# Copies at a layer's feed-forward boundary moved to ScalarE's queue, a bias formed on GpSimd, and the first norm's sum one product later

## The reference

```python
def rmsnorm(x, g): return x * rsqrt(mean(x * x) + eps) * g
mkv_p = mem_kv_proj(mem_prompt, w_mem_kv[i])             # memory keys and values of the prompt
hp, hs = rmsnorm(xp, norm_mix_pre[i]), rmsnorm(xs, norm_mix_pre[i])
# compression of cached keys/values: blocks of 32 rows to one token, through a hidden layer of 128
bias = einsum('jce,jcef->cf', pe, w1) + b1               # 32 positions j, key/value c, 64 features e
hid  = proj[:, :-1, :, 0] + proj[:, 1:, :, 1] + bias
ckv  = einsum('bnhcf,cfe->bnhce', gelu(hid), w2)
xp = xp + rmsnorm(mp @ w_out[i], norm_mix_post[i])
xp = xp + rmsnorm(swiglu_ffn(rmsnorm(xp, norm_ffn_pre[i]), w_ffn_in[i], w_ffn_out[i]), norm_ffn_post[i])
```

## Time and profile before

| | |
|---|---|
| median of 3 runs | 1276.94 us (1275.72 to 1277.89) |
| profiled execution | 1279.42 us |
| its span, first to last instruction | 1277.6 us |
| mean granted TensorE clock | 0.952 of full |
| PE busy | 1170.9 us, 92% of the span |
| PEld, DVE, ACT, POOL busy | 837.0, 357.8, 230.7, 223.0 us |
| DMA | 185.65 MB, 145 GB/s on average |
| longest waits of PE | 12.2 us for a `fi` slab, 11.9 us in three for VectorE, 11.5 us in 17 for ScalarE |

### The profile page before, as it was taken

The page is one execution under the profiler, slowest core; times in us unless marked ns, Lnnn a source line. Parts: engine busy times, 40 slices in busy tenths (PEclk is TensorE's granted clock), DMA queues, the critical chain, the costliest instruction groups (busy, mean ns, idle before and its releaser), DMA issues. The chain is left out here.

```text
span 1277.6 us, 16640 instructions
## 1 busy us (share of the span) xinstructions
PE 1170.9 (92%) x6096; PEld 837.0 (66%) x6096; DVE 357.8 (28%) x780; ACT 230.7 (18%) x546; POOL 223.0 (17%) x297
## 2 busy tenths in 40 slices
PE   6999999999789999999999979987649899999996
PEld 5766666667667777777777753334537677777774
DVE  5428776410221111000331054326501321111002
ACT  2411000003210000000222045553301210001000
POOL 0008667510001000100000051302440010000000
PEclk9999999999989999999999869998778899999998
DMA  6835433412943434644422451445541143343342
GB/s 271 326 99 188 135 99 119 131 50 99 344 188 132 135 138 142 275 136 136 165 99 100 157 175 49 130 142 198 161 136 67 66 165 132 133 135 123 126 138 75
DMA packets 58532, 185.65 MB, mean 145 GB/s; under 512 B 8449, under 2 KB 39426, under 8 KB 47618
## 3 DMA queue, kind: packets, MB, share of 16 engines
q1 hardware_dynamic: 51890, 166.89, 38.0%
q0 software_dynamic: 6144, 12.59, 3.4%
q10 hardware_dynamic: 432, 5.24, 1.0%
HBM read 180.91 MB, written 10.02 MB: 149 GB/s over the span
## 5 line engine op out<-in xcount | busy, mean ns | idle before, releaser
L721 PE MATMUL banks<-normed,slabs 128*128 128x288 f32 x1408 | 347.6, 410 | 16.9 <-DMA slabs<-in_wfi 12.2
L721 PEld LDWEIGHTS banks<-normed,slabs 128*128 128x128 f32 x1408 | 270.4, 192 | 93.9 <-issue 17.7
L761 PE MATMUL banks<-hidden,slabs 128*128 128x288 f32 x704 | 171.2, 406 | 1.4 <-issue 1.4
L697 PE MATMUL banks<-arena,phase 128*128 128x384 f32 x512 | 171.0, 492 | 0.0
L761 PEld LDWEIGHTS banks<-hidden,slabs 128*128 128x128 f32 x704 | 133.6, 190 | 39.0 <-issue 2.3
L697 PEld LDWEIGHTS banks<-arena,phase 128*128 128x128 f32 x512 | 96.5, 191 | 65.1 <-issue 1.2
L1436 POOL TENSOR_TENSOR projected<-projected,rstd 128x288 f32<-128x288 f32 x44 | 34.9, 794 | 453.4 <-ACT projected L1208 453.4
L488 PE MATMUL banks<-normed,slabs 128*128 128x288 f32 (+1 forms) x416 | 106.7, 413 | 1.2 <-ACT normed L1141 1.2
L488 PEld LDWEIGHTS banks<-normed,slabs 128*128 128x128 f32 (+1 forms) x416 | 77.2, 189 | 25.6 <-issue 3.7
L1208 ACT ACTIVATE projected<-projected 128x288 f32<-128x288 f32 x44 | 19.5, 443 | 281.4 <-DVE projected L1555 281.4
L1508 DVE TENSOR_TENSOR normed<-normed 128x288 f32<-128x288 f32 x24 | 11.0, 458 | 199.1 <-ACT normed L1201 199.1
(11 more groups left out here) (306 smaller groups left out, 1118.7 us busy)
## 6 DMA issues: line engine op xcount, KB each, us to landing
slabs<-in_wfi SPq DMA_DIRECT2D x44, 1024.0 KB, 4.9
slabs<-in_w SPq DMA_DIRECT2D x25, 1024.0 KB, 4.7
arena<-in_cmp SPq DMA_DIRECT2D x128, 192.0 KB, 2.8
slabs<-in_wfo SPq DMA_DIRECT2D x32, 704.0 KB, 4.0
arena<-in_slck SPq DMA_DIRECT2D x64, 96.0 KB, 2.7
arena<-in_slck POOLq DMA_DIRECT2D x64, 96.0 KB, 2.6
out_win_old<-in_winold SPq DMA_DIRECT2D x1, 6096.0 KB, 22.4
arena<-in_slcv POOLq DMA_DIRECT2D x48, 96.0 KB, 2.6
```

The costliest lines, as they stand in the source:

```text
L697: ins = nc.tensor.matmul(out.rearrange("p h (g s) -> p h g s", s=8), W1S[:, c, a, j, :], PG[b % 2][:, :, c * 8 + j, :, :].rearrange("p g h ...
L721: return nc.tensor.matmul(BK[2 * (u % SLOTS) + c][:, 0:T], wt[:, k, c * P:c * P + P], Hn[:, k, :], start=(k == 0), stop=(k == KC - 1), ski ...
L761: ins = nc.tensor.matmul(BK[b][:, 0:T], wt[:, k, :], HD[:, 11 * kh + k, :], start=(kh + k == 0), stop=(kh * 11 + k == 21))
```

## The change

Three edits, and what they need:

1. `pre_sum(0)` is called after the third product of the memory projection, not after the second. ScalarE's root stands behind the first copy of slab 1.
2. GpSimd forms the position products: one product of 4096 elements, W1 times `pe` held constant over 128 elements, into `arena` 2048 to 6144, four additions that halve it, the last into `PER`. TensorE sums over partitions with two one-column products. ScalarE's copy of the row goes. SP waits for GpSimd before it loads the first pages, which land in the same part of `arena`.
3. The window copy and layer 1's memory keys and values are issued by ScalarE after the last copy of the S5 loop, in the order keys, values, values, window rows. In SP's list they are gone. SP's loop over the `fi` slabs is written out and issues the same loads.

```diff
+        PEP = AR[:, 2048:6144].rearrange("p (c q f) -> p c q f", c=2, q=16)
...
+        glu_in, pe_summed = sem("glu_in_ready"), sem("position_products_summed")
...                                              (mem_project, TensorE)
                         banks.filled(ins, key)
+                        hook(2 * s + t)
                     release(n, key)
-                    hook(s)
...                                              (cmp_bias, TensorE)
-                pe.wait_ge(w1_loaded, 16)
-                banks.fill(pe, "pe", 6)
-                for c in range(2):
-                    for a in range(2):
-                        for j in range(8):
-                            q = 16 * c + 8 * a + j
-                            ins = nc.tensor.matmul(BK[6][0:1, P * c:P * c + P], pr("pe")[:, q:q + 1], W1S[:, c, a, j, :],
-                                                   start=(a + j == 0), stop=(a * 8 + j == 15))
-                banks.filled(ins, "pe")
-            def cmp_bias_turn():
-                banks.wait_given(pe, "pe")
+                pe.wait_ge(pe_summed, 1)
                 banks.fill(pe, "peT", 6)
                 for c in range(2):
-                    ins = nc.tensor.matmul(BK[6][:, c:c + 1], PER[0:1, P * c:P * c + P], ones[0:1, 0:1], start=True, stop=True)
+                    ins = nc.tensor.matmul(BK[6][:, c:c + 1], PER[:, P * c:P * c + P], ones[:, 0:1], start=True, stop=True)
                 banks.filled(ins, "peT")
...
-            mem_project(0, hook=lambda s: pre_sum(0) if s == 0 else None)
+            mem_project(0, hook=lambda i: pre_sum(0) if i == 2 else None)
...
             s5_blocks()
+            mem_step(0, 6, 7)
             cmp_bias()
-            mem_step(0, 6, 7)
-            cmp_bias_turn()
             mem_step(0, 6, 8)
...                                              (ScalarE)
+            mem_evac(0, 1, 0)
             root(0)
-            for t in range(2):
-                mem_evac(0, 1, t)
+            mem_evac(0, 1, 1)
...
-            banks.take(act, "pe")
-            banks.give(A(PER[0:1, :], BK[6][0:1, 0:2 * P], ACT.Copy), "pe")
...
             values_out(B - 1)
+            act.dma_start(AR[:, 0:4096], memk_in[1]).then_inc(mk_loaded, 16)
+            for h in range(2):
+                act.dma_start(AR[:, 4096 + 2048 * h:6144 + 2048 * h], memv_in[1][:, 2048 * h:2048 * h + 2048]).then_inc(mv_loaded[h], 16)
+            act.dma_start(winold_out, winold_in).then_inc(stored, 16)
...                                              (GpSimd)
             query_blocks(0, 6)
+            pool.wait_ge(w1_loaded, 16)
+            pool.wait_ge(prm_loaded, 16)
+            ch.step(tt(PEP.rearrange("p c q f -> p (c q) f"), U[:, 0:4096].rearrange("p (q f) -> p q f", f=P),
+                       pr("pe").unsqueeze(2).to_broadcast([P, 32, P]), ALU.mult))
+            for n in (8, 4, 2):
+                ch.step(tt(PEP[:, :, 0:n, :], PEP[:, :, 0:n, :], PEP[:, :, n:2 * n, :], ALU.add))
+            tt(PER.rearrange("p (c f) -> p c f", c=2), PEP[:, :, 0, :], PEP[:, :, 1, :], ALU.add).then_inc(pe_summed, 1)
...                                              (SP)
+            sp.wait_ge(pe_summed, 1)
             load_pages(0)
...
             load_stage("out", 0, N_OUT_SLAB)
-            sp.dma_start(winold_out, winold_in).then_inc(stored, 16)
             banks.take(sp, ("hc", B - 1, 1))
-            sp.dma_start(AR[:, 0:4096], memk_in[1]).then_inc(mk_loaded, 16)
-            for h in range(2):
-                sp.dma_start(AR[:, 4096 + 2048 * h:6144 + 2048 * h], memv_in[1][:, 2048 * h:2048 * h + 2048]).then_inc(mv_loaded[h], 16)
...
-            load_stage("fi", 0, FI)
+            for u in range(FI):
+                load(FIRST["fi", 0] + u)
```

More of the change, by code:

```diff
@@ L331, in trunk_kernel @@
         carry0 = sem("s5_carry_cleared")
-        glu_in = sem("glu_in_ready")
+        glu_in, pe_summed = sem("glu_in_ready"), sem("position_products_summed")
         bu_full, bu_free = sem("s5_inputs_made"), sem("s5_inputs_taken")
```

## The result

The changed kernel took 1285.61 us in the median of 10 runs (1280.26 to 1288.49), the kernel before 1279.35 in the runs beside it (10, 1275.71 to 1284.01). The ratio is 1.0050, 95% interval 1.0036 to 1.0064: some 6.3 us slower.

What follows compares the result with a forecast made beforehand. TensorE was taken to bound the kernel. Terms -2.3 + 10.1 + 2.8 - 5.0 + 2.6 = +8.2 us took the profiled 1279.42 us to 1287.6, and the median of 1276.94 to 1285; range 1269 to 1291.

Steps and rivals of the forecast that it cites:

- Part 1: At the first norm: TensorE's 2.34 us of idling for VectorE's sum of squares goes, -2.3 us; bounds -3.0 and 0.
- Part 2, the place: At the third memory head: TensorE stands 10.1 us because GpSimd's products hold VectorE's S5 input matrix; bounds 0 and 13.3.
- the rival in which scalings are held as well: At the first memory head: GpSimd also holds VectorE's scalings, TensorE stands 13.3 or 11.7 us, total 1287; chance 0.22.
- The forecast's own mechanism: At the S5 input matrix: whole GpSimd instructions alternate with VectorE's two-source products, making the third head's maximum 11.3 us late.
- Part 2, the product's length: GpSimd's 4096-element product for the bias: 10.2 us, at 2.49 ns an element taken from its products of 512.
- Part 2, the clock: Behind the memory-head stall: TensorE's granted clock falls and costs 2.8 us more; 0 at least.
- Part 2, the end: Before the S5 loop: without the 64 bias products 5.0 us is gained, not 7.15, as the memory values' DMA is late next.
- Page loads: SP waits for GpSimd before batch 0's pages: with the stall, pages are issued by 75 and nothing is late.
- Part 3, the gain: Ahead of layer 0's feed-forward: the 12.22 us wait for its first slab falls to 4.60, -7.6 us.
- Part 3, the stall: In the output projection: slab 3 is held by the window rows' 65 KB packets, 7.4 us of waiting and 2.8 of clock.
- the forecast's upper bound: For the copies edit as a whole: forecast +2.6 us, bounds -7.6 and +5.
- those in which the copies or GpSimd are harmless: Copies don't hold slab 3: 1275, chance 0.18; GpSimd's long products don't hold VectorE: 1274.5, chance 0.13; neither holds: 1264, 0.09.

Runs made afterwards that it cites:

- c1_copies: Only the third edit, the copies issued by ScalarE, against the kernel before: 1284.16 us, ratio 1.0039 (1.0025 to 1.0052), 5.0 us slower.
- b1_bias: Only the second edit, the bias on GpSimd, against the kernel before: 1285.42 us, ratio 1.0052 (1.0039 to 1.0065), 6.2 us slower.
- b4_after_pairs: Only the bias edit, GpSimd held back until VectorE scaled the first two memory heads, against the kernel before: 1285.75 us, ratio 1.0047, 6.1 us slower.

## Why the prediction came out as it did

The total is close, +8.2 forecast and +6.3 measured, and that is in part luck. Against the parts measured alone the terms are off by -1.7 (Part 1, -4.0 for -2.3), -1.7 (Part 2, +6.2 for +7.9) and +2.4 us (Part 3, +5.0 for +2.6), which partly cancel. The kinds of loss are those forecast; Part 2's stall came at another place, by the mechanism that the prediction had as a rival.

- **Part 1** (forecast -2.3, alone -4.0 with an interval of 2.6 to 5.0). The idling went as forecast; the term counted that alone, from one execution, and left out the clock. In the eight profiled executions without Part 1 TensorE idles 1.7 to 2.9 us there and input products start between 29.3 and 31.2 us; in the four with it there is no idling and they start between 26.5 and 27.2. In two of the eight, that of before among them, the clock fell as well: granted 0.80 from 20.5 to 29 us, the second memory slab 8.08 and 8.76 us long. In the other six it stayed at 1.00 and the slab took 7.07.
- **Part 2, the place** (10.1 us at the third head). This step failed. The stall is 9.4 us at the first head's turn, the place of the rival in which scalings are held as well. I had let that rival stand at 0.22 because no row showed a scaling beside GpSimd. The 11.32 us pair shows it now. The Trainium skill, "SBUF — State Buffer", section "Who interferes with whom", has that rule, and the trace agrees with it. The forecast's own mechanism is true too: it decides when GpSimd starts 5 us later, and costs 9.0 us there. But it isn't what the changed kernel paid: there the S5 input matrix began at 52.61, when GpSimd was all but done, and most of its products kept their 0.55 us. That 10.1 came so near to 9.4 is luck: the place was wrong and GpSimd's product too long. With the product's true length the forecast's own path would have stalled some 6 us, by this estimate: in the run with GpSimd held back the wait was 8.97 us and the product that was caught at 45.73 had 7.0 us of GpSimd's ahead of it; in the changed kernel the matrix was due at 45.19 - 4.56 = 40.63, 3.6 us before GpSimd's product ended, so 3.4 us less.
- **Part 2, the product's length** (10.2 us). It took 7.03, 1.72 ns an element, where I had carried over 2.49 from a product of two full operands. Length and operand both seem to count: GpSimd's addition of 2048 elements with two full operands took 4.49 us (2.19 ns an element), and products of 512 with one operand held over 128 took 1099 ns in the mean in the run with short instructions, against 1273. With 10.2 us the rival would have stood for 11.7 to 13.3.
- **Part 2, the clock** (2.8). The 16 matrix instructions behind the wait took 5.92 us, against 4.05 for as many at full clock, and the turn 1.11 against 0.60: 2.4.
- **Part 2, the end** (-5.0, "the DMA is late next"). The size is near, -4.6 up to the S5 loop; the cause was not the DMA, so this step failed too. The memory values' second half lands at 80.16 + 5.8 = 86.0, and half of the products that start at 85.01, which need only the first half of the values, take 1.65 us of the 3.29, to 86.66. What ends last ahead of them is the sample tokens' head: its turn, called short work in the prediction, stands 1.78 us for VectorE's scaling (84.03), a wait that the 64 bias products used to cover. From the S5 blocks to the last value product it is 4.98 us in place of 10.98, 6.0 gained; then the products' 3.29 us, against 1.96, take 1.3 back. That is the clock: 0.60 from 84 to 86 us and 0.63 from 86 to 88.4. The clock also takes 1.7 us back in the loop's first products, a term the forecast lacks. Page loads held nothing, as forecast.
- **Part 3, the gain** (-7.6). Right: 4.57 us remain ahead of the feed-forward and the stretch gives 7.7.
- **Part 3, the stall** (7.4 us for the third slab, 2.8 of clock). Turns by packet are right, the slab is not. I had keys, values and the first two slabs done near 314, with the window rows beginning beside slab 3. But ScalarE's queue already served window rows beside slab 2 (316 to 318 us above). That slab is wanted two products earlier than slab 3, and TensorE stood 2.2 us ahead of the first slab's products as well. Idling is 8.6 us in the changed kernel and 10.6 in Part 3 alone; the 128 products took 35.75 us, against 31.20, so the clock's term is 4.6: some 1.9 behind the first slab's wait and 2.7 behind the second's, where the forecast had one wait. Alone the part costs 5.0, the forecast's upper bound.
- Of the rivals, those in which the copies or GpSimd are harmless fall with c1_copies, b1_bias and b4_after_pairs. The price of the first is borne out: copies made harmless give 7.6 to 8.9 us, as the earlier trace rows had it. Of GpSimd made harmless no run has the price, since the one that gains 4.4 us leaves out most of its work as well.

Open: why the slab issued at 305.35 gets no packet before 308 us (ScalarE's queue, which had started 6 us earlier, has all of them until then: 54 and 53 in the two microseconds ahead; in the kernel before, with nothing beside it, a slab issued at 300.90 had its first 8 before 302); and the 0.9 us between the sum of the parts and the whole, which their intervals cover.

## What to carry to other kernels

Work moved to an idle GpSimd isn't free while VectorE works: a long GpSimd instruction held VectorE's two-source products and scalings for its whole length, and what stood in line behind them, so count what VectorE has due in that stretch and price the wait with the clock behind it. What a background copy costs loads that are waited for was set here by its packet size, 65 KB against 4, and not by its bytes: split long rows, or leave it in the queue behind the loads. The price of a stall of 6 to 12 us on TensorE was its idle time plus 1.8 to 2.9 us lost to a lower clock after it.

## What the runs showed of the hardware

- A GpSimd product of 4096 elements with one operand held over 128 took 7.03 us (1.72 ns an element); an addition of 2048 with two full operands took 4.49 (2.19), and one product of 512 with two full operands takes 1273 ns (2.49).
- One-source scalings of VectorE on 256 float columns are held by a GpSimd instruction like two-source products (11.32 us for a pair of 0.61); the maximum that reads PSUM kept 0.68 us in the changed kernel at 48.84, while GpSimd's additions ran (0.69 in the earlier trace rows), and a reciprocal on 2 columns of SBUF kept 0.17 us at 37.40, inside GpSimd's product.
- Two DMA queues on the same engines moved packets in near equal number, also where one's are 65 KB: 12 and 13 packets in 2 us, 0.78 and 0.08 MB; 72 and 68 with 4 KB packets.
- After much the same idling at the first norm the clock fell in two executions of eight (after 2.34 and 1.93 us) and not in six (1.67 to 2.86 us): the length of the gap alone does not decide it.
